# Layer B's softmax denominators: taken from the exponentials' accumulation and spread by products with the identity, in place of products with ones

## Chip, cores and metric

One Trainium2 chip (trn2), one core. The metric is the device time of one execution in microseconds.

## The reference, cut to what matters

One step of a two-layer decoder: layer A with stick-breaking attention, layer B with dilated window attention over one shared set of keys and values, each followed by a mixture of experts. There are 512 prompt tokens and 8 sample tokens, width 1024, 16 query heads of 64 and 4 key/value heads, all in fp32. The change is in layer B's attention of the prompt tokens:

```
DILATED = ((128, 1), (512, 4), (2048, 16))
def local_attend(q, k, v, mask):
    ...
    s = jnp.where(mask[..., None, None, :, :], s, NEG_INF)
    lse = jax.nn.logsumexp(s, axis=-1)
    p = jnp.exp(s - lse[..., None])
    o = jnp.einsum('...hgqc,...che->...qhge', p.astype(v.dtype), v)
def combine_groups(outs, lses):
    w = jax.nn.softmax(jnp.stack(lses), axis=0).astype(outs[0].dtype)
    return jnp.einsum('gbth,gbthe->bthe', w, jnp.stack(outs))
```

The three groups' outputs, weighted by the softmax of their log-sum-exps, equal one softmax over all keys of the three groups together: a token's output is the sum of exp(s - m) v over the three groups, divided by the sum of exp(s - m), with one maximum m.

## The kernel before, in words

Layer B (`layer_b`, line 1413) works through its four key/value heads j = 0 to 3, each with four query heads, taken as two pairs. Group 0 (window 128, no dilation) is laid out by token blocks b of 128 tokens ("near" scores, up to 256 keys per block); groups 1 and 2 are laid out by the residue of the token number modulo 4, so that four blocks of 128 tokens hold each residue ("far" scores, 128 keys per block).

For each j the four engines run orders that are written out by hand and meet through semaphores only. TensorE (lines 1698 to 1754) turns queries and keys, makes the scores and, between them, projects chunks of the weights for the next units (`project`, line 1566; `ahead`, line 1686). For j=3 nothing is left to project, and `ahead` gives chunks of the output projection (line 321) up to the last scores and nothing after them. VectorE masks the scores (`soft`, 1849), finds their maxima, evicts the projections, and scales the weights that were loaded. GpSimd (`front`, 1991) does the norms and the rotation of the heads.

Then come the softmax weights in eight parts per j, i = 0 to 7, part i belonging to pair i // 4; the parts with i % 4 = 0, 1 are groups 1 and 2, those with i % 4 = 2, 3 the near scores of blocks 0, 1 and 2, 3. Each part goes through:

- ScalarE, `exps` (1776): the exponentials in place, with the negative maximum as a per-partition bias: 8 instructions of 128 columns in parts 0 and 1, 2 of 128 and 2 of 256 in part 2, 4 of 256 in part 3 (and the same in parts 4 to 7). 192 in all.
- TensorE, `turn_p` (1640, "turn"): transposes of the blocks of both heads into PSUM banks 4 to 7.
- ScalarE and VectorE, `p_copy` (1787 and 1889): one head each, from PSUM into `pT`. On ScalarE the copy of part i-1 stands behind the exponentials of part i.
- TensorE, `weigh` (1655): for every block (4, 4, 3, 4 in the four parts of a pair) and both heads, one product with the values `vo` into bank 2, and one with a 128x64 block of ones into bank 3. A head's result is 64 partitions of a bank. Bank 3 then holds the sum of the exponentials, the same on all 64 partitions of a head. `vo` and the ones are the stationary operand, `pT` is the moving one.

After part 3 and part 7 VectorE (`finish_pair`, 1898) takes the reciprocal of bank 3 (line 1901) and multiplies it with bank 2 (1902). The first `weigh` of the next pair waits for that (semaphore `s_oc`).

The order on TensorE in this stage:

```
                        turn_p(j, 0)
                        turn_p(j, 1)
                        weigh(j, 0)
                        ahead(2, 2)
                        turn_p(j, 2)
                        weigh(j, 1)
                        ahead(2, 3)
                        turn_p(j, 3)
                        weigh(j, 2)
                        turn_p(j, 4)
                        weigh(j, 3)
                        ahead(2, 4)
```

An fp32 product shows as two matmul records and two weight loads in the trace.

Of the kernel before, what the change touches and what calls it, by code (L numbers as in the profile page):

```python
# [9 lines left out]
ALU = mybir.AluOpType  # L10
# [123 lines left out]
def build(nc, a, outs):  # L134
# [10 lines left out]
    with ExitStack() as ctx:  # L145
        def sb(name, shape, dt=F32, to=ctx):
            return to.enter_context(nc.sbuf_tensor(name, shape, dt))
# [3 lines left out]
        def sem(name):  # L151
            live[-1].append(nc.alloc_semaphore(name=name))
            return live[-1][-1]
# [16 lines left out]
        def bank(b, n=1):  # L170
            return ps[:, 512 * b:512 * (b + n)]
# [1241 lines left out]
        def layer_b(norm, next_norm):  # L1413
# [12 lines left out]
            with ExitStack() as ph, nc.Block() as block:  # L1426
# [12 lines left out]
                mx = sb("mx", [128, NDIL, 4, 4], to=ph)  # L1439
                mo = sb("mo", [128, 2, 4, 4], to=ph)  # L1440
                mres = sb("mres", [128, 4, 4], to=ph)
                neg = sb("neg", [128, 2, 4, 4], to=ph)
                rsr = sb("rsr", [128, 4], to=ph)
                gcol = sb("gcol", [128, 2, KT], to=ph)
# [9 lines left out]
                    sem("b_" + n) for n in ("y_added", "x_turned", "xT_ready", "weight_gains_in", "head_gains_in", "gain_ready",  # L1454
                                            "rstd_out", "rstd_by_residue", "weights_scaled", "proj_done", "proj_copied", "rope_done",
                                            "k_doubled"))
                s_tb, s_tbc, s_qk, s_sev, s_m0, s_mr, s_mo, s_mi, s_nr, s_nn, s_ex, s_tp, s_pta, s_ptd, s_pv, s_oc = (
                    sem("b_" + n) for n in ("qk_turned", "qk_copied", "scores_done", "scores_read", "near_max", "far_max", "max_out",
                                            "max_in", "far_max_ready", "near_max_ready", "exp_ready", "p_turned", "p_copied_act",
# [95 lines left out]
                def _(pe):  # L1555
# [99 lines left out]
                    def weigh(j, i):  # L1655

                        pair, s, q = i // 4, i % 4, NPART * j + i
                        pe.wait_ge(s_pta, q + 1)
                        pe.wait_ge(s_ptd, q + 1)
                        if s == 0 and q:  # L1660
                            pe.wait_ge(s_oc, 2 * j + pair)
                        blocks = p_blocks(s)
                        for n, (g, b, lo, o) in enumerate(blocks):
                            cols = slice(b, SEQ, 4) if g else slice(128 * b, 128 * b + 128)
                            v = vo[:, j % 2, g, b if g or lo else b - 1, :]
                            for out, held in ((bank(2), v), (bank(3), ones[:, 0:HD])):
                                for h in range(2):
                                    last = nc.tensor.matmul(out[64 * h:64 * h + 64, cols], held, pT[:, q % 2, 512 * h + 128 * o:512 * h + 128 * o + 128],
                                                            start=(s == 0 and n == 0), stop=(s == 3 and n == len(blocks) - 1),
                                                            skip_group_check=True)  # L1670
                        last.then_inc(s_pv, 1)

                    turn_x(*TILES[0])
# [82 lines left out]
                @block.scalar  # L1756
                def _(act):
                    rows_back(act, 1)
                    for t, rows in TILES:
                        act.wait_ge(s_xt, t + 1)  # L1760
                        src = bank(2 + 2 * (t % 3), 2).rearrange("p (k m) -> p k m", k=KT)
                        nc.scalar.activation(xT[:, :, 128 * t:128 * t + rows], src[:, :, 0:rows], ACT.Copy).then_inc(s_xc, 1)
                        norm.square(act, t, junk)

                    def turned(j, g):

                        n = 3 * j + g
                        act.wait_ge(s_rope, n + 1)
                        nc.scalar.activation(tok[:, g, 0:4, 0:HD], tok[:, g, 0:4, HD:2 * HD], ACT.Copy).then_inc(s_kk, 1)
                        for f in range(3):  # L1770
                            act.wait_ge(s_tb, 3 * n + f + 1)
                            if f == 0 and n:
                                act.wait_ge(s_qk, NSTEP * j + STEP0[g])
                            nc.scalar.activation(kT[:, :] if f == 2 else qT[:, f, :], bank(6 + f % 2), ACT.Copy).then_inc(s_tbc, 1)

                    def exps(j, i):

                        pair, s = i // 4, i % 4
                        act.wait_ge(s_nn if s >= 2 else s_nr, j + 1)
                        for h in (2 * pair, 2 * pair + 1):  # L1780
                            for b in range(4) if s < 2 else (2 * s - 4, 2 * s - 3):
                                g = (1, 2, 0, 0)[s]
                                v = sc[g][:, h, b, :] if g or b else sc[0][:, h, 0, 128:256]
                                last = nc.scalar.activation(v, v, ACT.Exp, bias=neg[:, 0 if g else 1, b, h:h + 1])  # L1784
                        last.then_inc(s_ex, 1)

                    def p_copy(j, i):

                        q = NPART * j + i
                        act.wait_ge(s_tp, 2 * q + 1)  # L1790
                        if q >= 2:
                            act.wait_ge(s_pv, q - 1)
                        lo = 128 if i % 4 == 2 else 0
                        nc.scalar.activation(pT[:, q % 2, lo:512], bank(6 - 2 * (i % 2))[:, lo:512], ACT.Copy).then_inc(s_pta, 1)

                    for j in range(NKV):
                        for g in range(NDIL):
                            turned(j, g)
                        exps(j, 0)
                        for i in range(1, NPART):  # L1800
                            exps(j, i)
                            p_copy(j, i - 1)
                        p_copy(j, NPART - 1)

                @block.vector
                def _(dve):
# [82 lines left out]
                    def p_copy(j, i):  # L1889
# [5 lines left out]
                        lo = 128 if i % 4 == 2 else 0  # L1895
                        V.tensor_copy(pT[:, q % 2, 512 + lo:1024], bank(7 - 2 * (i % 2))[:, lo:512]).then_inc(s_ptd, 1)

                    def finish_pair(j, pair):

                        dve.wait_ge(s_pv, NPART * j + 4 * pair + 4)  # L1900
                        dve_do(V.reciprocal(orec, bank(3)))
                        V.tensor_tensor(oT[:, 2 * j + pair, 0:SEQ], bank(2), orec, ALU.mult).then_inc(s_oc, 1)
# [19 lines left out]
                    for j in range(NKV):  # L1922
                        more = j < NKV - 1

                        def ahead(u, c):
                            if u == 0:
                                evict(j, 2, c)
                            elif more:
                                evict(j + 1, u - 1, c)
                            elif (u, c) in GIVEN:  # L1930
                                out_b.add(dve, 0, GIVEN[u, c], at=0)

                        if more:
                            scale(j + 1, 0)
                        ahead(0, 0)
                        ahead(0, 1)
                        soft(j, 0, 0)
                        ahead(0, 2)
                        soft(j, 0, 1)
                        ahead(0, 3)  # L1940
                        soft(j, 0, 2)
                        ahead(0, 4)
                        soft(j, 0, 3, s_m0)
                        ahead(0, 5)

                        ahead(1, 0)
                        ahead(1, 1)
                        soft(j, 1, 0)
                        ahead(1, 2)
                        soft(j, 1, 1)  # L1950
                        ahead(1, 3)

                        if more:
                            scale(j + 1, 1)
                        ahead(1, 4)
                        ahead(1, 5)
                        soft(j, 2, 0)
                        ahead(2, 0)
                        soft(j, 2, 1)
                        far_max(j)  # L1960
                        ahead(2, 1)

                        p_copy(j, 0)
                        near_max(j)
                        p_copy(j, 1)
                        ahead(2, 2)
                        p_copy(j, 2)
                        ahead(2, 3)
                        p_copy(j, 3)
                        p_copy(j, 4)  # L1970
                        finish_pair(j, 0)
                        ahead(2, 4)
                        p_copy(j, 5)
                        p_copy(j, 6)
                        if more:
                            scale(j + 1, 2)
                        ahead(2, 5)
                        p_copy(j, 7)
                        finish_pair(j, 1)
# [241 lines left out]
```

## Time and profile before

| | us |
|---|---|
| median of 3 runs | 1603.14 |
| lowest, highest | 1596.12, 1603.99 |
| the profiled execution | 1603.43 |
| its span in the profile | 1601.4 |
| TensorE busy, of the span | 1354.0 (85%) |
| VectorE, ScalarE, GpSimd busy | 626.5, 325.8, 441.7 |

Layer B with its attention lies between 640 and 1187 us of the span, its sample tokens between 1187 and 1280, and the second mixture of experts after that. All times below are microseconds from the start of the span. Engines: PE is TensorE's matmul, PEld its weight load, DVE VectorE, ACT ScalarE, POOL GpSimd, SP SyncE.

### The profile page before, as it was taken

The page shows a single profiled execution, that of the slowest core. Times are in us where ns is not written, and L with a number is a line of the kernel's source. Part 1 is how long each engine was busy: PE and PEld are TensorE (multiplying, and loading weights), DVE is VectorE, ACT ScalarE, POOL GpSimd, SP SyncE. Part 2 cuts the span into 40 slices and gives each one's busy share as a digit, 9 for nine tenths or more (in the row PEclk, how much of TensorE's full clock was granted, in tenths as well). Part 3 has the DMA queues.
Part 4 walks back from the last instruction along what each step waited for, and adds up shares of the span by engine and source line. Part 5 has one row for each costly group of instructions (what it writes and reads, how often), then busy time and mean ns, then how long its engine had stood idle before and what let it go on. Part 6 is the DMA issues. An engine that isn't in the chain of part 4 may idle for free. (4 is left out here: it accounts for less than half of the span.)

```text
span 1601.4 us, 20133 instructions
## 1 busy us (share of the span) xinstructions
PE 1354.0 (85%) x8138; PEld 943.1 (59%) x8138; DVE 626.5 (39%) x869; ACT 325.8 (20%) x633; POOL 441.7 (28%) x378
## 2 busy tenths in 40 slices
PE   5899999986899888399999999999953669999882
PEld 5577887436566555268577677685541266665451
DVE  2376764424211111244546445544337641111113
ACT  3223223111222111110141140230320102222110
POOL 3222332010111110039746837836100001111110
PEclk9999999995899999799999999999985658999997
DMA  7945342309799999541220131111036097999994
GB/s 254 328 139 173 124 144 95 120 4 369 282 420 420 420 421 414 186 122 42 54 75 15 47 82 46 48 42 34 8 93 175 12 379 299 420 420 420 421 402 179
DMA packets 149508, 326.26 MB, mean 204 GB/s; under 512 B 57880, under 2 KB 103416, under 8 KB 124736
## 3 DMA queue, kind: packets, MB, share of 16 engines
q1 hardware_dynamic: 134432, 287.21, 48.1%
q0 software_dynamic: 13824, 33.84, 5.8%
q10 hardware_dynamic: 1184, 4.26, 0.7%
q8 instruction: 47, 0.77, 0.2%
q14 instruction: 21, 0.17, 0.0%
HBM read 307.48 MB, written 34.29 MB: 213 GB/s over the span
## 5 line engine op out<-in xcount | busy, mean ns | idle before, releaser
L1579 PE MATMUL ps<-wB,xT_b 128*128 128x384 f32 x768 | 263.4, 497 | 9.0 <-DVE wB L1824 8.8
L933 PE MATMUL ps<-wg,oT 128*64 128x256 f32 x1024 | 237.2, 385 | 19.3 <-DMA wd<-in_w_down 17.6
L933 PE MATMUL ps<-wu,oT 128*64 128x256 f32 x1024 | 237.5, 386 | 0.0
L1579 PEld LDWEIGHTS ps<-wB,xT_b 128*128 128x128 f32 x768 | 204.0, 271 | 53.2 <-DVE wB L1824 9.2
L933 PEld LDWEIGHTS ps<-wg,oT 128*64 128x64 f32 x1024 | 139.8, 139 | 74.6 <-DMA wd<-in_w_down 27.7
L478 PE MATMUL ps<-xnT_a,wA 128*128 128x260 f32 (+1 forms) x768 | 173.1, 386 | 2.1 <-DMA wA<-in_w_qkv_a 1.3
L478 PEld LDWEIGHTS ps<-xnT_a,wA 128*128 128x128 f32 x768 | 145.8, 191 | 28.0 <-issue 5.1
L933 PEld LDWEIGHTS ps<-wu,oT 128*64 128x64 f32 x1024 | 139.7, 139 | 37.0 <-issue 16.4
L1333 POOL DMA_INDIRECT y_rows<-ysb,idx x32 | 32.1, 1003 | 435.5 <-DVE ysb L968 419.8
L951 PE MATMUL ps<-wd,hT 128*64 128x512 f32 x512 | 124.0, 601 | 30.4 <-DVE hT L962 30.4
L959 DVE TENSOR_TENSOR h<-sg,ps 64x256 f32<-64x256 f32 x64 | 26.4, 413 | 236.8 <-ACT sg L956 236.8
L329 PE MATMUL ps<-wB,oT 128*128 128x512 f32 x128 | 70.4, 701 | 44.2 <-DVE x L337 38.5
L968 DVE COPY ysb<-ps 64x512 f32<-64x512 f32 x64 | 44.4, 693 | 137.1 <-PE ps L951 137.1
L221 POOL TENSOR_TENSOR ss<-ss,cst 128x1 f32<-128x1 f32 (+1 forms) x20 | 5.7, 286 | 263.7 <-ACT junk_s L213 128.2
L951 PEld LDWEIGHTS ps<-wd,hT 128*64 128x64 f32 x512 | 36.6, 136 | 70.2 <-issue 70.2
L1784 ACT ACTIVATE arena_b<-arena_b,neg 128x128 f32<-128x128 f32 (+1 forms) x192 | 64.1, 417 | 50.7 <-DVE neg L1881 49.6
L329 PEld LDWEIGHTS ps<-wB,oT 128*128 128x128 f32 x128 | 26.5, 218 | 81.2 <-DVE x L337 47.1
L1997 POOL TENSOR_TENSOR sq<-tok 128x1600 f32<-128x1600 f32 x12 | 34.2, 2852 | 135.7 <-DVE tok L1847 135.7
L965 ACT ACTIVATE ysb<-ps 64x512 f32<-64x512 f32 x64 | 37.7, 589 | 152.4 <-PE ps L951 152.4
L811 POOL TENSOR_TENSOR work<-work,cst 128x512 f32<-128x512 f32 x32 | 49.4, 1565 | 66.8 <-ACT work L636 66.8
L956 ACT ACTIVATE sg<-ps 64x256 f32<-64x256 f32 x64 | 24.3, 380 | 210.8 <-PE ps L933 184.2
L790 POOL DMA_INDIRECT vres<-in_cache_kv_a,gidx x32 | 33.3, 1040 | 120.0 <-DVE gain_row L699 100.3
(259 smaller groups left out, 2051.8 us busy)
## 6 DMA issues: line engine op xcount, KB each, us to landing
wg<-in_w_gate SPq DMA_DIRECT2D x64, 1024.0 KB
wu<-in_w_up SPq DMA_DIRECT2D x64, 1024.0 KB
wd<-in_w_down SPq DMA_DIRECT2D x64, 1024.0 KB
wA<-in_w_qkv_a SPq DMA_DIRECT2D x24, 512.0 KB, 4.6
wB<-in_w_q_b SPq DMA_DIRECT2D x12, 1024.0 KB, 7.2
wB<-in_w_kv_b SPq DMA_DIRECT2D x24, 256.0 KB, 4.0
work<-in_w_qkv_a SPq DMA_DIRECT2D x1, 4096.0 KB
vres<-qa_rows SPq DMA_DIRECT2D x8, 512.0 KB, 4.5
```

The lines of the kernel that those rows point to most:

```text
L329: last = nc.tensor.matmul(bank(at + n)[0:TILES[t][1], :], oT[:, m, 128 * t:128 * t + TILES[t][1]], self.w[m][:, 512 * n:512 * n + 512], st ...
L478: last = nc.tensor.matmul(bank(6 + h)[:, 0:half], wA[:, m, k, :], xnT[:, k, half * h:half * h + half], start=(k == 0), stop=(k == KT - 1))
L790: pool.indirect_dma_start(out=dst, out_offset=None, in_=cache_rows, in_offset=bass.IndirectOffsetOnAxis(ap=gidx[:, kind, u:u + 1], axis=0) ...
L811: nc.gpsimd.tensor_tensor(d, d, C("below").unsqueeze(1).unsqueeze(1).to_broadcast([128, 2, 2, 128]), ALU.mult).then_inc(s_msk, 1)
L933: last = nc.tensor.matmul(bank(q)[lo:lo + CAP, 0:FE], x[:, k, :], wt[:, k, :], start=(k == 0), stop=(k == KT - 1))
L951: last = nc.tensor.matmul(bank(4 + q)[CAP * n:CAP * n + CAP, :], hT[:, q, f, :], wd[s][:, f, 512 * n:512 * n + 512], start=(f == 0), stop= ...
L965: return nc.scalar.activation(ysb[w][CAP * q:CAP * q + CAP, 0:512], bank(4 + q)[0:CAP, :], ACT.Copy)
L968: return nc.vector.tensor_copy(ysb[w][CAP * q:CAP * q + CAP, 512:D], bank(4 + q)[CAP:2 * CAP, :])
L1333: pool.indirect_dma_start(out=y_rows, out_offset=rows_of(idx, 1, v), in_=ysb[v % 2][:, :], in_offset=None, bounds_check=2 * TOK - 1, oob_i ...
L1579: last = nc.tensor.matmul(bank(c % 2)[:, 0:UW], xT[:, kt, cols], wB[:, g, kt, :], start=(kt == 0), stop=(kt == KT - 1))
L1784: last = nc.scalar.activation(v, v, ACT.Exp, bias=neg[:, 0 if g else 1, b, h:h + 1])
L1997: pool_do(P.tensor_tensor(sq[:, :, :], kq, kq, ALU.mult))
```

## The change

The exponentials also write out their row sums (`accum_out`), so that each of the 192 instructions leaves a column of 128 sums in `sums` (by group, block and head). VectorE adds the sums of groups 1 and 2 (`far_sums`), four blocks and two heads at a time, once per pair. The products with ones are gone from `weigh`. In their place, at the end of part 3 of a pair, TensorE makes eight products per head: for each near block and each far block the column of sums, spread over 64 columns by a stride of zero, is the stationary operand and the identity is the moving one, so that the 128 sums come out along the free axis on all 64 partitions of the head, and near and far add up in bank 3.

```diff
+                sums = sb("sums", [128, NDIL, 4, 4], to=ph)
+                far_sums = sb("far_sums", [128, 4, 4], to=ph)
...
+                s_fs = sem("b_far_sums")
...
                         for n, (g, b, lo, o) in enumerate(blocks):
                             cols = slice(b, SEQ, 4) if g else slice(128 * b, 128 * b + 128)
                             v = vo[:, j % 2, g, b if g or lo else b - 1, :]
-                            for out, held in ((bank(2), v), (bank(3), ones[:, 0:HD])):
-                                for h in range(2):
-                                    last = nc.tensor.matmul(out[64 * h:64 * h + 64, cols], held, pT[:, q % 2, 512 * h + 128 * o:512 * h + 128 * o + 128],
-                                                            start=(s == 0 and n == 0), stop=(s == 3 and n == len(blocks) - 1),
-                                                            skip_group_check=True)
+                            for h in range(2):
+                                last = nc.tensor.matmul(bank(2)[64 * h:64 * h + 64, cols], v, pT[:, q % 2, 512 * h + 128 * o:512 * h + 128 * o + 128],
+                                                        start=(s == 0 and n == 0), stop=(s == 3 and n == len(blocks) - 1),
+                                                        skip_group_check=True)
+                        if s == 3:
+                            pe.wait_ge(s_fs, 2 * j + pair + 1)
+                            for held, near in ((sums[:, 0], True), (far_sums, False)):
+                                for b in range(4):
+                                    for h in range(2):
+                                        last = nc.tensor.matmul(bank(3)[64 * h:64 * h + 64, slice(128 * b, 128 * b + 128) if near else slice(b, SEQ, 4)],
+                                                                held[:, b, 2 * pair + h:2 * pair + h + 1].to_broadcast([128, HD]), ident,
+                                                                start=(near and b == 0), stop=(not near and b == 3), skip_group_check=True)
                         last.then_inc(s_pv, 1)
...
-                                last = nc.scalar.activation(v, v, ACT.Exp, bias=neg[:, 0 if g else 1, b, h:h + 1])
+                                last = nc.scalar.activation(v, v, ACT.Exp, bias=neg[:, 0 if g else 1, b, h:h + 1],
+                                                            accum_out=sums[:, g, b, h:h + 1])
...
+                    def add_far_sums(j, pair):
+
+                        dve.wait_ge(s_ex, NPART * j + 4 * pair + 2)
+                        hs = slice(2 * pair, 2 * pair + 2)
+                        V.tensor_tensor(far_sums[:, :, hs], sums[:, 1, :, hs], sums[:, 2, :, hs], ALU.add).then_inc(s_fs, 1)
...
                         p_copy(j, 1)
+                        add_far_sums(j, 0)
...
                         p_copy(j, 5)
+                        add_far_sums(j, 1)
                         p_copy(j, 6)
```

## Rows read from the trace of the kernel before

**Rows 1.** By stretch: busy us (instructions) of each engine, granted clock, DMA share, GB/s.
```profile
918.00:960.00 42.00, 38.65 (x366) 32.77 (x365) 17.89 (x26) 20.14 (x58) 16.29 (x11) 1.00 0.30 79
...
1149.00:1187.00 38.00, 28.56 (x308) 23.27 (x307) 15.51 (x21) 19.39 (x56) 0.00 (x0) 0.90 0.01 1
...
1280.00:1601.00 321.00, 252.76 (x1697) 167.74 (x1695) 77.12 (x166) 55.13 (x103) 32.42 (x32) 0.89 0.90 367
```

**Rows 2.** Timeline, j=3, and the start of the sample stage.
```profile
1149.81 4.78 ACT L1784 ACTIVATE arena_b<-arena_b,neg 128x128 f32<-128x128 f32 x16 [15.24 <-DVE neg L1881]
...
1163.78 0.44 PE L1668 MATMUL ps<-arena_b,vo 128*64 128x128 f32 x4
...
1165.68 1.09 PE L1651 MATMUL ps<-cst,arena_b 128*128 128x128 f32 x8
...
1170.02 0.69 PE L1668 MATMUL ps<-arena_b,vo 128*64 128x128 f32 x4 [3.25 <-DVE oT L1902]
...
1178.88 0.39 PE L1668 MATMUL ps<-arena_b,vo 128*64 128x128 f32 x4
...
1181.28 0.39 PE L1668 MATMUL ps<-arena_b,cst 128*64 128x128 f32 x4
1181.71 3.36 DVE L1901 RECIPROCAL gain_row<-ps 128x512 f32<-128x512 f32 x1 [2.53 <-PE ps L1668]
...
1186.27 5.29 PE L329 MATMUL ps<-wB,oT 128*128 128x512 f32 x8 [4.61 <-PEq L1426]
```

**Rows 3.** Groups by form, 800 to 1190 us: busy us, mean ns, idle before.
```profile
L1668 PE MATMUL ps<-arena_b,cst 128*64 128x128 f32 x480 | 48.6, 278 | 0.0
...
L1784 ACT ACTIVATE arena_b<-arena_b,neg 128x128 f32<-128x128 f32 x144 | 45.0, 390 | 50.7 <-DVE neg L1881 49.6 <-DVE neg L1887 1.1
...
L1668 PEld LDWEIGHTS ps<-arena_b,cst 128*64 128x64 f32 x480 | 32.1, 141 | 0.0
...
L1784 ACT ACTIVATE arena_b<-arena_b,neg 128x256 f32<-128x256 f32 x48 | 21.5, 498 | 0.0
```

**Rows 4.** Timeline of ScalarE: accumulator reads, and what follows them.
```profile
690.76 0.19 ACT L213 ACTIVATION_READ_ACCUMULATOR sq<-x 128x1 f32 x1
690.85 1.01 ACT L1762 ACTIVATE xT_b<-ps 128x1024 f32<-128x1024 f32 x1
...
1255.83 0.51 ACT L2171 ACTIVATE pr<-pr,sml 128x256 f32<-128x256 f32 x1 [6.38 <-DVE sml L2138]
1256.24 0.19 ACT L2171 ACTIVATION_READ_ACCUMULATOR pr<-pr,sml 128x1 f32 x1
1256.34 1.04 ACT L213 ACTIVATE junk_s<-x 128x1024 f32<-128x1024 f32 x1
```

**Rows 5.** Timeline, j=1, to weigh 4: start, us, instructions, [idle before <- releaser].
```profile
918.04 0.17 DVE L1880 TENSOR_TENSOR neg<-mres,mo 128x16 f32<-128x16 f32 x1
...
918.46 4.79 ACT L1784 ACTIVATE arena_b<-arena_b,neg 128x128 f32<-128x128 f32 x16 [11.90 <-DVE neg L1881]
...
923.30 1.09 PE L1651 MATMUL ps<-cst,arena_b 128*128 128x128 f32 x8 [1.25 <-ACT arena_b L1784]
...
925.97 1.70 ACT L1784 ACTIVATE arena_b<-arena_b,neg 128x256 f32<-128x256 f32 x4
...
926.22 5.55 PE L1579 MATMUL ps<-wB,xT_b 128*128 128x384 f32 x16
...
940.27 0.60 ACT L1794 ACTIVATE arena_b<-ps 128x512 f32<-128x512 f32 x1 [5.32 <-PE ps L1651]
...
946.41 1.09 PE L1651 MATMUL ps<-cst,arena_b 128*128 128x128 f32 x8
...
949.33 0.44 PE L1668 MATMUL ps<-arena_b,vo 128*64 128x128 f32 x4 [1.82 <-DVE oT L1902]
```

**Rows 6.** As rows 1, in stretches of 2 us behind the wait before weigh 4, j=3.
```profile
1170.00:1172.00 2.00, 1.98 (x19) 2.00 (x21) 0.47 (x1) 0.00 (x0) 0.00 (x0) 0.50 0.00 0
...
1174.00:1176.00 2.00, 2.00 (x16) 1.67 (x16) 0.56 (x1) 0.49 (x1) 0.00 (x0) 0.53 0.00 0
```

## The prediction

> **What bounds the kernel now.** I read first the busy time by stretches [rows 1]. In the attention stage of layer B TensorE is busy for 38.65 of 42 us where the softmax weights of kv head j=1 (four heads) are used, between projections. Only the last such stretch, j=3, has no projection in it, and there it is busy for 28.56 of 38 us. What follows, the sample tokens and then the last mixture of experts (DMA share 0.90), starts behind a barrier at the end of this stage (1186.27 [rows 2]), so a microsecond saved or lost in the stage moves the end by one.
>
> Then the groups by form [rows 3]: the products with `ones` are 480 records, two for each of 240 products (8 pairs of heads, 15 blocks, 2 heads). Their durations overlap; the price is the distance between starts. In the timeline of j=3 [rows 2] groups of four records (one block, both heads), of `vo` and of `ones` in turn, follow each other from 1178.88 to 1181.28 with 11 steps: 2.40/11 = 0.218 us. I call this one slot.
>
> **What the change removes and adds on TensorE.** A pair loses 15 slots of `ones` (4, 4, 3, 4 in its four parts) and gets 8 with the identity, all at the end of part 3. So parts 0, 1, 2 get shorter by 0.87, 0.87, 0.65 us and part 3 longer by 4 slots, 0.87. Net 7 slots = 1.53 us a pair, 12.2 us over 8 pairs. That the new products (stationary: one column spread over 64; moving: identity) cost a slot is an assumption; no row has such a stationary operand. The nearest are the `vo` and `ones` slots [rows 2], which don't differ although one reads fresh data and the other constants. Low bound 0.218 us (the form is the same, nothing could make it less), high bound two slots, if the two heads no longer ran side by side: 64 x 0.218 = 14 us more.
>
> Against this price the Trainium skill has a rule: "TensorE: Matmul & The Clock Gate", Part 3, says that a weight load overlaps running matmuls only if it goes to other rows of the array, and all loads here use all 128 rows. By it each of the four records would also pay its load (0.141 us in [rows 3]), 4 x (0.141 + 0.055) = 0.78 us a slot, the 56 slots saved would be 44 us and the sum near 1560. The trace disagrees with four starts in 0.218 us, so the rule gets no share of the chances.
>
> **What it adds on ScalarE.** Each of the 192 exponentials gets a read of the accumulator. Such a read is 186 ns in its row, but starts before its activation ends, and the next activation starts 0.09 us (690.76 to 690.85) and 0.10 us (1256.24 to 1256.34) after it [rows 4]. The Exp of 256 columns there starts 0.41 us before its read, as far as two follow each other without one: four take 1.70 us [rows 5] and one 0.498, so (1.70-0.498)/3 = 0.40 from start to start. For 128 columns it is (4.79-0.39)/15 = 0.293 [rows 3, 5]. So I take 0.10 us more for each: 0.395 and 0.505. Bounds: 0 (a read wholly hidden) and 0.576 and 0.684 (390+186, 498+186 ns end to end). I take the low value because the read rows are the same instruction at work. A part of eight narrow ones then releases its waiters after 7 x 0.395 + 0.297 + 0.186 = 3.25 us where it was 2.44, two parts in a row after 6.41 where it was 4.78 (+1.63). Part 2 takes 1.89 (1.49), part 3 takes 2.11 (1.69).
>
> **Who waits for that.** For j=0..2 the order on TensorE is: turn part 0, turn part 1, weigh 0, projection, turn 2, weigh 1, projection, turn 3, weigh 2, turn 4, weigh 3. Turn 1 already waits for the exponentials (923.30 [rows 5]), and turn 0 for its half of them. After the change turn 1 starts 1.63 us later. ScalarE's next release, part 2, then comes by 927.3, and turn 2 stands behind 5.5 us of projection (926.22 [rows 5]), so it isn't delayed. Part 5 is the next tight one: behind the copy at 940.27 it starts about 940.8 and ends at 944.1, and its reader stood at 946.41 [rows 5]. The other end, the reciprocal (3.36 us [rows 2]), starts when weigh 3 ends and holds back weigh 4 (949.33 [rows 5]): this wait is fixed and just moves. Pair 1 has no exponential that is awaited. So for one j: pair 0 gains 1.53 and loses 1.63, pair 1 gains 1.53: -1.43 us, times three -4.3. I round to -4.2 for the semaphore behind the read.
>
> j=3 has no projections as cover. Followed with the same durations from 1149.81 [rows 2] (a turn of eight blocks takes 1.0, a copy 0.5 before what stands behind it on ScalarE): parts 0 and 1 end 1156.2, turn 1 starts 1156.3 (was 1154.6), weigh 0 ends 1158.3, part 2 ends 1158.5, turn 2 and weigh 1 end 1160.4, part 3 ends 1161.0, turn 3 and weigh 2 end 1162.9, part 4 (from 1161.3) ends 1164.55, turn 4 ends 1165.6, weigh 3 with 12 slots for 8 (it took 1163.78 to 1165.68 = 1.90, so 2.77) ends 1168.4. It was 1165.68 [rows 2]: +2.7 us, because ScalarE has become the chain from part 2 on. Then the reciprocal, weigh 4 at 1172.7 (was 1170.02). Behind this 3.25 us wait the granted clock was 0.50 (1.2 GHz of 2.4) until about 1175.9 [rows 6]. If it is so again, weigh 4, turn 6 and weigh 5 take 1.9, 1.5 and 1.9, turn 7 1.0, weigh 6 0.8, weigh 7 2.77: the reciprocal starts 1182.8 where it was 1181.71. j=3 costs +1.1.
>
> The rest: eight additions of 128x8 on VectorE, after the copies of parts 1 and 5. The nearest row, 128x16, is 0.17 us (918.04 [rows 5]). Their semaphore has been passed by then, and VectorE next evicts or copies what TensorE makes only after the 5.5 us projection, in j=3 after turn 2. Cost 0; without this cover 1.4 us. TensorE's new wait stands two parts after that addition: 0. No DMA is issued anew, and none of SP's or POOL's steps is passed. POOL's chain and the weight loads start from TensorE's results and move with them.
>
> **Sum.** -4.2 + 1.1 = -3.1 us. The profiled execution is 1603.43 (span 1601.4), the median of the runs shown 1603.14; so 1600.3 us, -0.2%. 0.5% (8 us) is about what a measurement of this kernel can tell from no change.
>
> **Rivals.**
> (a) Slower: the reads run end to end. Place: exponentials of parts 0 and 1, and the whole ScalarE chain of j=3. For j<3 turn 1 waits 16 x 0.576 - 4.78 = 4.4 us more, against 3.06 gained: +1.4 each, +4.1. In j=3 weigh 3 ends at about 1174.0, +8.3, and pair 1 gives back 1.7: +6.6. Together +10.7: 1614. It decides once a read costs more than about 0.14 us (then the sum passes zero). Against it: all read rows [rows 4]. For it: they follow one wide activation, not eight narrow ones. 0.09.
> (b) Slower: the clock. The wait before turn 1 grows from 1.3 to about 2.1 us. If the granted clock fell to half behind it as it did behind the 3.25 us [rows 6], and came back 5.9 us later, 2.9 us would be added in each of j=0..2 and up to as much in j=3, which has such a stretch already: -3.1 + 8.8 to 11.7 = 1609 to 1612, say 1610. It decides as soon as two of the four waits do it. Against it: the 1.82 us wait at 949.33 [rows 5] left the clock at 1.00 in the stretch of j=1 [rows 1]. 0.06. The Trainium skill, same page, "Why this matters for your kernels", warns of gaps in TensorE's work in mid-kernel as what brings the half clock back; the trace agrees for the long wait and not for the short.
> (c) Slower: the spread column is dear (two slots): -3.1 + 14 = 1614. 0.07.
> (d) Faster: reads hidden. Then j<3 gains 3.06 each, 9.2, and j=3 about 2.5: 1591.7. Against it: the 0.10 us at 1256.34 [rows 4]. 0.08.
> (e) The forecast, 0.70; a tenth of it may leave the band by noise or small errors (the three runs shown spread over 7.9 us).
>
> **Numbers.** Faster by over 0.5% (below 1595): (d) and 0.05 of (e), 0.13. Slower (above 1611): (a), (c), a part of (b), 0.18. Same 0.69. The range, 1591 to 1611, holds (e) but for its edges, (d) and most of (b), and leaves out (a) and (c).
>
> **What would show it.** No 480-record group that names `cst` beside `arena_b` on the weighing line, and 256 records with `sums` and `far_sums`. 192 reads of 186 ns, sixteen exponentials of parts 0 and 1 in 6.3 to 6.4 us, turn 1 held 1.6 us longer, weigh 3 four slots longer, weigh 0 four shorter, the reciprocal of j=3 starting 1.1 us later against the start of its exponentials. Wrong if those sixteen take 9 us (a), if the clock leaves 1.00 before 1149 (b), if a slot of the new products takes over 0.22 us (c).

## The result, and the profile after

The changed kernel takes 1608.66 us (median of 20 runs, 1602.12 to 1613.31) against 1602.40 (20 runs, 1596.12 to 1608.87): ratio 1.0038, interval 1.0026 to 1.0050. Forecast was 1600.3, a gain of 3.1 us. The median lies in the range of 1591 to 1611, but the change costs about 6 us (by the interval 4.2 to 8.0) where it should have saved 3.

I read the stage by one number that the noise of other stages doesn't touch: **S**, from the first exponential of j=0 to the first product of the sample stage. Before it is 1186.27 - 806.40 = 379.87 us, after 1192.16 - 806.43 = 385.73. So 5.9 us are made there, of 7.0 between these two profiled executions (1603.43 and 1610.45) and 6.3 between the medians. A second number is the start of the reciprocal (the end of a pair's weighing), counted from the first exponential of its j: before, 26.64 and 40.84 us for the two pairs of j < 3, so 14.20 from one to the other.

Groups by form in the changed kernel, 800 to 1195 us, and below it the timeline of j=1 (the columns of [rows 3] and [rows 5]). Line 1794 has the exponentials, 1654 the turns, 1670 the `vo` products, 1678 the new ones, 1907 VectorE's copies, 1918 the reciprocal:

```profile
L1794 ACT ACTIVATE arena_b<-arena_b,neg 128x128 f32<-128x128 f32 x144 | 55.6, 389 | 49.7 <-DVE neg L1892 49.7
...
L1794 ACT ACTIVATION_READ_ACCUMULATOR arena_b<-arena_b,neg 128x1 f32 x192 | 36.5, 190 | 0.0
...
L1678 PE MATMUL ps<-cst,far_sums 128*64 128x128 f32 x128 | 8.5, 273 | 0.0
L1678 PE MATMUL ps<-cst,sums 128*64 128x128 f32 x128 | 8.5, 273 | 0.0
```

```profile
923.19 1.09 PE L1654 MATMUL ps<-cst,arena_b 128*128 128x128 f32 x8 [0.95 <-ACT arena_b L1794]
926.27 1.41 PE L1654 MATMUL ps<-cst,arena_b 128*128 128x128 f32 x8 [1.99 <-ACT arena_b L1794]
927.61 1.98 PE L1670 MATMUL ps<-arena_b,vo 128*64 128x128 f32 x16
...
946.05 1.04 PE L1678 MATMUL ps<-cst,sums 128*64 128x128 f32 x16
946.92 1.04 PE L1678 MATMUL ps<-cst,far_sums 128*64 128x128 f32 x16
...
948.01 3.36 DVE L1918 RECIPROCAL gain_row<-ps 128x512 f32<-128x512 f32 x1 [2.09 <-PE ps L1678]
...
955.78 2.29 DVE L1835 TENSOR_TENSOR wB<-wB,gcol 128x2048 f32<-128x2048 f32 x1
...
957.98 0.60 DVE L1858 TENSOR_SCALAR tok<-ps,rs 8x384 f32<-8x384 f32 x1
958.51 0.67 DVE L1907 COPY arena_b<-ps 128x512 f32<-128x512 f32 x1
...
959.33 1.09 PE L1670 MATMUL ps<-arena_b,vo 128*64 128x128 f32 x16 [1.59 <-DVE arena_b L1907]
```

The reads and the new products are what was forecast: sixteen records of new products (four slots) start 0.87 us apart from the next sixteen, 0.218 a slot. The exponentials of j=3, instruction by instruction:

```profile
1155.19 0.39 ACT L1794 ACTIVATE arena_b<-arena_b,neg 128x128 f32<-128x128 f32 x1
1155.49 0.19 ACT L1794 ACTIVATION_READ_ACCUMULATOR arena_b<-arena_b,neg 128x1 f32 x1
1155.58 0.39 ACT L1794 ACTIVATE arena_b<-arena_b,neg 128x128 f32<-128x128 f32 x1
```

0.385 us from one to the next, where 0.293 was without a read: 0.09 for a read whose row says 190 ns. Two things are not in the forecast's sum. First, `weigh 7` now waits 1.59 us for VectorE's copy, which stands behind the scaling of the next weights and an eviction (the last rows of the timeline). In the kernel before it already waited 0.28 us for the same copy, as its timeline shows (line 1824 is the scaling, 1847 the eviction, 1896 the copy; PEld is TensorE's weight load):

```profile
952.61 3.41 DVE L1824 TENSOR_TENSOR wB<-wB,gcol 128x1024 f32<-128x1024 f32 x2
...
955.95 0.60 DVE L1847 TENSOR_SCALAR tok<-ps,rs 8x384 f32<-8x384 f32 x1
...
956.47 0.67 DVE L1896 COPY arena_b<-ps 128x512 f32<-128x512 f32 x1
...
956.84 0.39 PE L1668 MATMUL ps<-arena_b,cst 128*64 128x128 f32 x4
957.26 0.23 PEld L1668 LDWEIGHTS ps<-arena_b,vo 128*64 128x64 f32 x4 [0.28 <-issue]
957.29 0.44 PE L1668 MATMUL ps<-arena_b,vo 128*64 128x128 f32 x4
```

Second, behind the 1.99 us wait of turn 1 the clock goes to its lower level, 1.2 of 2.4 GHz (stretches as in [rows 1]; the third last number is the granted clock):

```profile
924.00:926.00 2.00, 0.28 (x3) 0.04 (x1) 1.21 (x3) 2.00 (x11) 1.92 (x2) 1.00 1.07 252
926.00:928.00 2.00, 1.73 (x12) 1.41 (x14) 0.28 (x1) 2.00 (x10) 2.00 (x1) 0.72 1.04 344
928.00:930.00 2.00, 2.00 (x17) 1.67 (x14) 1.02 (x2) 2.00 (x8) 1.84 (x3) 0.50 0.19 66
930.00:932.00 2.00, 2.00 (x7) 1.66 (x7) 0.00 (x0) 0.89 (x4) 1.76 (x4) 0.92 0.02 6
```

`weigh 0` with four slots takes 1.91 us (927.61 to 929.52), as long as eight took before. In j=2 the clock fell once more, behind the wait for the reciprocal, and pair 1 took 42.92 - 28.09 = 14.83 us.

### The profile page after: what moved, and what is told of

It reads as the page before. It is cut to its first block and busy times, and to the rows that moved or that the text cites. A ratio compares the mean times of both kernels' runs of the same rounds, so it can differ in the third digit from the quotient of the medians.

```text
span 1608.3 us, 19885 instructions
## 1 busy us (share of the span) xinstructions
PE 1351.4 (84%) x7914; PEld 938.4 (58%) x7914; DVE 625.9 (39%) x877; ACT 343.2 (21%) x825; POOL 441.5 (27%) x378
## 5 line engine op out<-in xcount | busy, mean ns | idle before, releaser
L1794 ACT ACTIVATE arena_b<-arena_b,neg 128x128 f32<-128x128 f32 (+1 forms) x192 | 79.2, 417 | 49.7 <-DVE neg L1892 49.7
```

## The experiments

All are edits of the changed kernel unless said otherwise; "before" is the kernel before. Theory 1 is VectorE's scaling ahead of the copy of part 7, theory 2 the clock behind the longer wait. The runs were taken in several sessions, each with executions of the kernel before beside it (medians 1603.88, 1602.60 and 1601.63 us); the ratio is to those, so compare ratios and not medians. S and the reciprocals are of one profiled execution each.

| run | us (median) | ratio to before, interval | S | reciprocals of j = 0, 1, 2: pair 0 / pair 1 |
|---|---|---|---|---|
| before | 1602.40 | | 379.9 | 26.64, 26.64, 26.64 / 40.84, 40.83, 40.84 |
| changed | 1608.66 | 1.0038 (1.0026, 1.0050) | 385.7 | 28.11, 28.06, 28.09 / 42.31, 42.25, 42.92 |
| scaling last | 1617.30 | 1.0087 (1.0071, 1.0103) | 394.0 | 28.12, 28.06, 28.21 / 44.49, 44.42, 46.15 |
| before, scaling last | 1618.32 | 1.0101 (1.0086, 1.0117) | 393.1 | 26.64, 26.64, 26.65 / 44.74, 44.73, 44.74 |
| filled wait | 1604.50 | 1.0006 (0.9997, 1.0016) | 382.2 | 26.60, 26.59, 26.60 / 42.04, 40.78, 42.03 |
| projection first, scaling last | 1602.16 | 0.9998 (0.9983, 1.0014) | 382.5 | 23.22, 23.22, 23.22 / 41.15, 41.15, 39.59 |
| scaling early | 1605.20 | 1.0018 (1.0003, 1.0034) | 379.1 | 26.59, 28.05, 28.12 / 39.26, 40.72, 40.79 |
| projection first, scaling early | 1590.25 | 0.9916 (0.9900, 0.9932) | 366.5 | 23.21, 23.22, 23.23 / 37.45, 35.89, 37.46 |
| before + accumulator outputs | 1616.89 | 1.0087 (1.0070, 1.0105) | 387.9 | 28.12, 29.74, 28.12 / 42.32, 43.94, 42.32 |
| new products on constants | 1598.05 | 0.9962 (0.9950, 0.9974) | 372.9 | 25.11, 25.11, 25.12 / 39.31, 39.94, 39.31 |
| before, projection first, scaling early | 1597.09 | 0.9966 (0.9950, 0.9982) | 371.6 | 24.65, 24.61, 24.60 / 38.57, 38.53, 38.52 |
| before, scaling early | 1603.15 | 0.9999 (0.9985, 1.0013) | 377.8 | 26.64, 26.64, 26.64 / 40.56, 40.56, 40.56 |
| scaling early, filled wait | 1598.29 | 0.9976 (0.9961, 0.9992) | 373.5 | 26.60, 26.60, 26.60 / 39.27, 39.27, 39.27 |
| projection first, scaling early, j=3 pair 0 plain | 1587.83 | 0.9896 (0.9874, 0.9917) | 365.7 | 23.22, 23.22, 23.22 / 37.47, 35.89, 37.45 |

**Scaling last**, in the changed kernel and in the one before:

```diff
-                        if more:
-                            scale(j + 1, 2)
                         ahead(2, 5)
                         p_copy(j, 7)
+                        if more:
+                            scale(j + 1, 2)
```

> The changed kernel with one step of VectorE moved: the scaling of the next weights (3.4 us) goes from ahead of the eviction and the copy of part 7 to behind that copy, for j=0..2. Measure S: from the first exponential of j=0 to the first product of the sample stage (before 379.9 us, changed 385.7). Theory 1: in the changed kernel weigh 7 waits 1.6 us for the copy of part 7, which stands behind that scaling; the four and three slots saved in weigh 5 and weigh 6 are lost there. Then weigh 7 starts about 1.5 us earlier in each of three j, S falls by 4.6 to about 381.1, and the time to about 1604. Rival: the wait belongs to something else that comes just as late (ScalarE's copy, or the accumulator reads): S stays at 385 to 386.

> The same move of the scaling in the kernel before, as a control. Theory 1: there weigh 7 waits only 0.28 us for that copy, so S (379.9) falls by at most 0.9, to 379.0, and the time is within 0.1% of before. If the move itself were worth more, S would fall by over 2.

Both missed by far, and for the same reason. The wait of weigh 7 did go (its products follow those of weigh 6 in one row of 28 records, and the first turn for the next j comes 1.5 us earlier from the first exponential), but the scaling now ran beside GpSimd and took 6.88 us for 3.4; TensorE waited 2.8 us for it in the changed kernel and 3.3 in the one before, and the clock fell each time. The groups of both engines in the changed kernel with the scaling last, 958 to 968 us:

```profile
L1835 DVE TENSOR_TENSOR wB<-wB,gcol 128x2048 f32<-128x2048 f32 x1 | 4.0, 3967 | 0.0
...
L1835 DVE TENSOR_TENSOR wB<-wB,gcol 128x1024 f32<-128x1024 f32 x1 | 3.0, 2987 | 0.0
```

```profile
L2019 POOL TENSOR_TENSOR sq<-sq 128x400 f32<-128x400 f32 x1 | 3.0, 2955 | 0.1
...
L2019 POOL TENSOR_TENSOR sq<-sq 128x800 f32<-128x800 f32 x1 | 2.7, 2744 | 0.1
```

In the changed kernel as it was, the narrower scaling takes 1.2 us and GpSimd's two additions 1.04 and 1.88. Each held the other up. The Trainium skill has it ("SBUF — State Buffer", "Who interferes with whom"): a VectorE instruction with two inputs in SBUF contends with a GpSimd one that reads SBUF. The trace agrees, 3.0 us for 1.2 and 2.96 for 1.04. So the scaling is better off ahead of the eviction that starts GpSimd. These two runs tell nothing on theory 1's price, and the place had to be another.

**Filled wait**: eight products of constants ahead of turn 1, into a bank that turn 1 overwrites.

```diff
+                        if i == 1:
+                            pe.wait_ge(s_sev, NSTEP * j + NSTEP)
+                            for _ in range(8):
+                                nc.tensor.matmul(bank(4)[:, 0:128], ident, ones, start=True, stop=True)
                         pe.wait_ge(s_ex, q + 1)
```

> The changed kernel with eight 128x128x128 products of constants (8 x 0.218 = 1.75 us) on TensorE in the 2.0 us wait ahead of turn 1, into a bank that turn 1 overwrites. Theory 2: behind this wait the granted clock falls to 0.50 in each j and turn 1, weigh 0 and the start of the projection run at half speed, 1.3 us a j. With the wait filled the clock stays 1.00, the reciprocal of pair 0 starts 26.7 to 26.8 us after the first exponential (28.06 in the changed kernel, 26.64 before), and S falls by 4 to 5, to about 381. Rival (the wait costs only itself and the rest comes from elsewhere, say from the new products): S stays at 385.7 or grows by what the fillers add.

Theory 2 is shown for pair 0: 28.1 became 26.60 in all three j, and the clock is 1.00 through the same place. The timeline of TensorE there, in j=1:

```profile
919.28 1.95 PE L1649 MATMUL ps<-cst 128*128 128x128 f32 x16
921.43 1.09 PE L1658 MATMUL ps<-cst,arena_b 128*128 128x128 f32 x8 [0.20 <-ACT arena_b L1798]
922.45 1.09 PE L1674 MATMUL ps<-arena_b,vo 128*64 128x128 f32 x16
923.48 0.71 PE L1582 MATMUL ps<-wB,xT_b 128*128 128x384 f32 x1
```

Adding work made the kernel about 5 us faster (ratio 1.0006 for 1.0038). In j=0 and 2 the 1.8 us wait for the reciprocal then brought the half clock in pair 1 (42.04 - 26.60 = 15.4 us, where 14.2 is the undisturbed length), so S fell by 3.5 and not by 4 to 5.

**Projection first**, here with the scaling last, which spoils pair 1:

```diff
+                        ahead(2, 2)
                         turn_p(j, 0)
                         turn_p(j, 1)
                         weigh(j, 0)
-                        ahead(2, 2)
...
+                        near_max(j)
+                        ahead(2, 2)
                         p_copy(j, 0)
-                        near_max(j)
                         p_copy(j, 1)
                         add_far_sums(j, 0)
-                        ahead(2, 2)
```

> The changed kernel with the scaling moved as above, and with the first projection chunk of this stage (5.5 us on TensorE) put ahead of turn 0 instead of behind weigh 0, VectorE's near maximum and its eviction of that chunk ahead of the first copy. Theories 1 and 2 together: the waits ahead of turn 0 (0.95) and turn 1 (1.98) go, the clock stays up (1.3), weigh 7 doesn't wait (1.5): 5.8 us in each of three j, S about 368.5, the time about 1591.5. Rival: the waits come back elsewhere, at turn 2 for the exponentials of part 2 or at the reciprocal: S above 376.

Pair 0 did what was expected, 4.84 us less; pair 1 lost it to the scaling beside GpSimd, and S came to 382.5 for the 368.5 expected.

**Scaling early**, behind the copy of part 2, where VectorE waits for a projection and GpSimd is idle; alone, and with the projection first:

```diff
                         p_copy(j, 2)
+                        if more:
+                            scale(j + 1, 2)
                         ahead(2, 3)
...
-                        if more:
-                            scale(j + 1, 2)
                         ahead(2, 5)
```

> The changed kernel with the scaling of the next weights moved the other way, ahead: behind VectorE's copy of part 2, where VectorE waits 6 us for a projection and GpSimd's chain has ended. S is 385.7 in the changed kernel, 379.9 before. Theory 1: weigh 7's wait of 1.6 us goes and nothing is pushed into GpSimd's time; each j<3 falls from 113.5 to about 112.0, S by 4.6 to 381.1. Rival: the gain goes again into another wait or into the clock, S above 384.

> The same, and the first projection chunk ahead of turn 0, near maximum and that eviction ahead of the first copy (as in the earlier run, whose reciprocal of pair 0 started 23.22 us after the first exponential, 4.84 earlier than the changed kernel's). Theories 1 and 2: 4.84 + 1.5 us off each of three j, S = 385.7 - 19 = 366.7, the time about 1590. Rival: the waits for the reciprocal (1.8 us) bring the half clock in pair 1, where TensorE now has less work around them, S above 370.

Theory 1 is shown: pair 1 takes 39.26 - 26.59 = 12.67 us for 14.20, in each j. S fell by 6.6 rather than 4.6, by chance of the clock: in this execution it didn't fall in j=0 (1.5 us), nor in pair 1 of j=2 (0.6). The medians moved by less, ratio 1.0018 for 1.0038. Together with the projection first the kernel is 0.84% faster than before; it was expected at about 1590 and took 1590.25. That is closer than the reasoning deserves: in j=0 and 2 the rival came true and the half clock cost pair 1 1.57 us (14.24 where j=1 took 12.67), and j=3 was 2.5 us shorter than in the changed kernel, since the clock stayed up behind its 3.25 us wait, and the expectation hadn't counted that.

**Each half alone**: the accumulator outputs on the kernel before, and the new products with `ones[:, b:b + 1]` in place of the sums.

> The kernel before with the accumulator outputs alone: the 192 exponentials write their sums, nobody reads them, and the products with ones stay. Theory: the reads hold turn 1 for 1.6 us more and this wait brings the half clock (1.3 us), 2.9 to 3.1 us in each j<3, about 2.5 in j=3: S from 379.9 to about 391, the time to about 1614. Rival: the reads cost only the 1.6 us: S about 387.

> The changed kernel without accumulator outputs and without VectorE's additions: the sixteen new products per pair take constant columns of ones, so the softmax denominators are left out of the computation; the products' number, form and place are the changed kernel's. Theory 1: pair 0 gains its 1.53 us and pair 1 none (weigh 7 waits for the copy behind the scaling): -1.5 in each j<3 and about -2 in j=3, S about 373.5. If the new products were dearer than a slot of 0.218 us, S would be near 380; if pair 1 gained too, 369.

This second kernel leaves the softmax denominators out of the computation. The new products are worth what theory 1 said, 7.0 us of S: 1.53 in pair 0 of each j < 3 and 3.0 in j=3, less 0.6 for the half clock in j=1. Pair 1 gains nothing: in j=0 and 2 weigh 7 waits 1.59 us for the copy, and in j=1 0.7 us, where the half clock had slowed TensorE ahead of it. TensorE's waits in that j, 916 to 963 us (sum, count, longest, in us):

```profile
PE ps L1670 <- DVE oT L1917: 1.8, 1, 1.8
PE ps L1654 <- ACT arena_b L1793: 1.5, 2, 1.2
PE ps L1670 <- DVE arena_b L1905: 0.7, 1, 0.7
```

The outputs alone cost 8.0 us of S in the profiled execution (11 were expected) and 14 us in the median. Pair 0 lost 1.48 in j=0 and 2 and 3.10 in j=1: the half clock came in one of the three. The gap to the median isn't explained in full. This execution was the fastest of five (1607.36), and its first exponential stood at 801.3 us, 5 us earlier than before's, for a reason outside the stage: from 300 to 400 us its granted clock was 0.83 for 0.78. Over the whole span it had a mean granted clock of 0.929, the other four 0.921 to 0.923, so they spent more time at the lower level; in which places is not shown.

**Controls and the forecast's own sum.**

> The kernel before (ones products, no accumulator outputs) in the order that brought the changed kernel from S = 385.7 to 366.5: the first projection chunk ahead of turn 0, the scaling behind the copy of part 2. Theory: before, the waits ahead of turn 0 and 1 are 0.2 and 1.25 us in each j<3 and weigh 7's 0.28; they go, so S falls by about 3 x 1.9 to 374, the time to about 1597. The change would then be worth 374 - 366.5 = 7.7 us once nothing stands in its way (two pairs of 1.53 in each of three j would be 9.2, less what j=3 loses). Rival: the order alone is what helps and the change is worth nothing in it either: S about 367.

> The kernel before with the scaling alone moved behind the copy of part 2, the control to the same move in the changed kernel. Theory 1: weigh 7 waits there only 0.28 us for the copy behind the scaling, so S falls by at most 0.9, to 379.0, the time within 0.1% of before.

> The changed kernel with the scaling moved ahead and the wait ahead of turn 1 filled with eight constant products. Both losses taken away, the reads and the new products left: the forecast's own sum. Theories 1 and 2: the reciprocal of pair 0 at 26.6 and of pair 1 at 39.2 to 39.3 us after the first exponential (26.64 and 40.84 before), 1.5 us less than before in each j<3, j=3 at most 1 more: S about 376, the time about 1600. If the wait for the reciprocal (1.8 us) brings the half clock in pair 1 in some j, as in the run with the filler alone, each costs 1.2 us more.

> The best so far (S = 366.5, 1590 us) with pair 0 of the last j as it was before: no accumulator outputs and ones products there, since ScalarE is the chain there and TensorE waits. The reciprocal of that pair started 18.36 us after the first exponential with the reads and 15.97 without. Theory: it comes at 16 to 17, and S falls by 1.5 to 2.4, to 364 to 365, less what the clock gives or takes; the time 1588 to 1589. Rival: the wait just moves to pair 1's exponentials: S 366 to 367.

With both losses taken away (scaling early, filled wait) the clock is 1.00 over the whole of j < 3, as one stretch of that run shows:

```profile
806.00:1145.00 339.00, 323.55 (x1925) 240.84 (x1924) 163.96 (x206) 90.74 (x348) 191.36 (x145) 1.00 0.17 47
```

Each j takes 110.48 us for 112.06: 1.58 less, where the forecast had 1.43. But 0.28 of it is the early scaling's own, as the same move in the kernel before shows (111.77 a j, and nothing to see in the time), so the change itself gives 1.3. In pair 1 it gives 1.25 and not 1.53, since weigh 7 waits 0.28 us for VectorE's copy even here: the copy (0.69 us) follows turn 7, and weigh 6 with three slots (0.65) doesn't cover it.

```profile
952.57 2.04 PE L1674 MATMUL ps<-arena_b,vo 128*64 128x128 f32 x28
952.68 0.69 DVE L1911 COPY arena_b<-ps 128x512 f32<-128x512 f32 x1 [0.41 <-PE ps L1658]
...
953.48 0.88 PEld L1674 LDWEIGHTS ps<-arena_b,vo 128*64 128x64 f32 x16 [0.28 <-issue]
```

The median is 0.24% below the kernel before, near the 0.2% of the forecast's sum. S fell by more, 6.3 us, because j=3 was spared the half clock behind its 3.25 us wait and took 1.6 us less where 1.1 more was forecast.

The order with the projection first is good for the kernel before too, 0.34%, 2.3 us a j for the 1.9 expected. The change is worth another 5.1 us of S in this order and 0.5% of the time; 7.7 us was expected, and the half clock in pair 1 of j=0 and 2 took 3.1 of them. So the waits and the clock were what it lost to. In the last run, with the lowest median, the first reciprocal of j=3 stands at 15.98 us for 18.36; since pair 1 gave most of it back, S fell by only 0.8, and the interval overlaps that of the run without this step:

```diff
+                                if j == NKV - 1 and pair == 0:
+                                    last = nc.scalar.activation(v, v, ACT.Exp, bias=neg[:, 0 if g else 1, b, h:h + 1])
```

(with the products with ones kept there in `weigh`). It is 1.0% faster than the kernel before, by the ratios 1.4% faster than the changed one.

**How often the clock falls.** Three single executions, of the changed kernel (1607.64 and 1600.37 us) and the one before (1603.44):

> The changed kernel again, for the clock alone. In its first profile the half clock came behind the 2.0 us wait ahead of turn 1 in all four j; in the run with accumulator outputs alone it came in two of four, in the one with the scaling moved ahead in three. If it is certain with this wait, the reciprocal of pair 0 starts 28.1 us after the first exponential in all three j<3, S 385.7. If it depends on something that differs between executions, some j show 26.6 and S is 1.5 us lower for each.

> The same once more, with the same two readings: 28.1 in all j<3 and S 385.7, or 26.6 in some and S lower by 1.5 for each.

> The kernel before again. Its waits of 1.25 us (turn 1) and 1.8 us (the reciprocal) left the clock at 1.00 in its first profile. If they never bring the half clock, the reciprocals stand at 26.6 and 40.8 us in all j<3 and S is 379.9 again; if they do in some executions, one of the two is later by 1.2 to 1.5 us, and the kernel before pays for the clock too.

The changed kernel twice had 26.60, 29.23 to 29.26 and 28.05 us for pair 0 (S 384.3 both times): no loss in j=0, 2.6 us in j=1, 1.5 in j=2. The kernel before had 26.65 and 42.46 in j=0, a half-clock stretch behind the 1.8 us wait, and S 380.4. So neither wait is safe or fatal. Over its three profiled executions the changed kernel lost 4.1 to 4.5 us in pair 0 of j < 3 and 0.3 to 0.6 in pair 1; the kernel before lost nothing in one and 1.6, in pair 1, in the other.

That the changed kernel spends more time at the lower level isn't a matter of three executions only: its mean granted clock was 0.922 over the 20 measured ones, against 0.927 to 0.928 over the 75 of the kernel before that were measured beside the experiments. With the wait filled it was 0.928 (11 executions); with the scaling early 0.921, and with both 0.927 (12 each).

Counted over all seventeen traces, j < 3, these are the waits of TensorE and how often the granted clock fell to 0.50 within them or up to 1.6 us behind:

| wait, us | where | fell |
|---|---|---|
| 1.25 | turn 1, without reads | 0 of 15 |
| 1.6 | weigh 7 | 0 of 9 |
| 1.8 | weigh 4, for the reciprocal | 14 of 51 |
| 2.0 | turn 1, with reads | 13 of 18 |
| 2.8 to 3.3 | projection, scaling last | 9 of 9 |

The places differ in more than the length of the wait, so this is a count and not a rule. The fourteen falls behind the reciprocal's wait are one in 18 where the old products with ones follow and thirteen in 33 where the shorter weighing does; why isn't tested.

In the first of the three, the timeline of the same turns in j=2:

```profile
1036.34 1.09 PE L1654 MATMUL ps<-cst,arena_b 128*128 128x128 f32 x8 [0.96 <-ACT arena_b L1794]
1039.42 1.61 PE L1654 MATMUL ps<-cst,arena_b 128*128 128x128 f32 x8 [1.98 <-ACT arena_b L1794]
```

and in the kernel before, its stretches of j=0 behind the wait for the reciprocal (columns as in [rows 1]):

```profile
835.00:837.00 2.00, 0.68 (x10) 0.71 (x12) 1.97 (x4) 1.27 (x4) 0.00 (x0) 0.93 1.07 239
837.00:839.00 2.00, 2.00 (x23) 2.00 (x21) 0.23 (x1) 0.00 (x0) 0.00 (x0) 0.50 0.99 280
```

## Why the prediction was wrong

- **Slots of the new products: right.** 0.218 us; rival (c) is out (new products alone, 0.9962).
- **Price of a read: right.** 0.09 us a step against 0.10 taken; rivals (a) and (d) are out.
- **Pair 0 of j < 3: right but for the clock.** Forecast +0.10 us, measured -0.04 where the clock stayed (26.60 for 26.64). Turn 1 starts 1.48 us later from the first exponential (6.32 for 4.84) where 1.63 was forecast; half of it is waited ahead of turn 0 (0.95 for 0.21), half ahead of turn 1 (1.99 for 1.25).
- **"Pair 1 has no exponential that is awaited", so it "gains 1.53": the step that failed.** I followed ScalarE and TensorE through pair 1 and left out the third engine. VectorE's chain there, copy of part 6, scaling 3.41, eviction 0.60, copy of part 7, was already what weigh 7 waited for, by 0.28 us, so whatever shortens weigh 5 and weigh 6 only lengthens that wait. The four slots of weigh 4 are passed on, because VectorE's chain starts from turn 6 behind it, and are spent on the four that weigh 7 has more; the seven of weigh 5 and 6, 1.53 us, are lost. The pair takes 14.20 us before and after. Loss against the sum: 3 x 1.53 = 4.6 us.
- **Rival (b), with 0.06, was the other half.** I held that a 1.82 us wait had left the clock alone and so a 2.1 us one would. One execution doesn't show that: another of the same kernel lost the clock behind the 1.82 us wait. The price was 2.9 us a stretch; it measured 1.5, in two cases 2.6. Loss: 4.1 to 4.5 us in pair 0. The Trainium skill's warning of gaps ("TensorE: Matmul & The Clock Gate", "Why this matters for your kernels"), which I had set against that row, speaks of longer gaps than these. The filled wait bears it out for 2.0 us: with the gap gone, so was the half clock.
- **j=3: right in size.** The second reciprocal was 0.9 us later in the first profiles (32.80 for 31.89), and in the single executions 32.03 and 32.06 for 30.77, against +1.1. The half clock behind its waits came and went here too, so one pair of executions couldn't have shown it.
- **What a measurement can tell.** I took 8 us for the least that shows. With 20 executions of each the interval is 2 us to either side, and a loss of 6 is clear of zero.

In the first profile the terms add up: pair 0 of three j -0.1, the clock in pair 0 +4.5, in pair 1 of j=2 +0.6, j=3 +0.9, together 5.9 us, which is what S shows. The two single executions have 4.4 against the first profile before. All lie in the interval of the medians, 4.2 to 8.0 us. The clock's part is a chance of each execution; the mean granted clock of the 20 says that more time at the lower level is usual for the changed kernel, not what it costs in the mean.

## What to carry to other kernels

When a step gets shorter on the engine that bounds, list for each step behind it what all the others are doing at that moment and how much each has to spare; a chain that ends 0.3 us behind the one you shorten is the bound already. If such a chain is in the way, move its long instruction to where the engine idles, but look what else runs there: the same 3.4 us took 6.9 beside GpSimd. Here waits of about two microseconds on TensorE could cost twice their growth, since the clock fell behind many of them: useful work ahead of them (here a projection chunk) removed the wait and the clock's loss at once, and with the scaling moved as well a 0.4% loss became a 0.8% gain, of which 0.3% is due to the new order and 0.5% to the change.

## What was not expected of the hardware

- Eight needless products (1.75 us) in a 2.0 us wait made the changed kernel 0.3% faster, about 5 us, since the granted clock stayed at 1.00 behind it.
- The same 2.0 us wait brings the half clock in one execution and not in another (13 of 18 over all traces), and a stretch costs 1.5 or 2.6 us.
- VectorE's scaling and GpSimd's additions stretched each other from 1.2 to 3.0 and from 1.04 to 2.96 us.
